# Mixture-of-experts scatter: one fp32 matmul with a weighted matrix, or two fp32r matmuls with a 0/1 matrix

## The reference

```python
    w = pg_top * pe_top / jnp.sum(pe_top, axis=-1, keepdims=True)
    eid = g_sel * EXP_PER_GROUP + e_sel
    combine = jnp.sum(jax.nn.one_hot(eid, N_EXPERTS, dtype=f32) * w[..., None], axis=1)
    hid = jax.nn.silu(jnp.einsum('td,edf->tef', t, w1)) * jnp.einsum('td,edf->tef', t, w3)
    hid = hid * combine[..., None].astype(hid.dtype)
    out = jnp.einsum('tef,efd->td', hid, w2)
    ...
    x = x + hier_moe(rms_norm(x, norm2_g), ...)
    return rms_norm(x, final_g)
```

## Time and profile before

| | us |
|---|---|
| median of 3 runs | 1282.17 (1280.4 to 1282.84) |
| span of the profiled execution | 1279.8 |
| PE busy | 1226.5 (96%) |
| DVE busy | 642.7 (50%) |
| ACT busy | 417.0 (33%) |
| DMA over the span | 263 GB/s mean |

### The profile page before, as it was taken

The page is one execution under the profiler, slowest core; times in us unless marked ns, Lnnn a source line. Parts: engine busy times, 40 slices in busy tenths (PEclk is TensorE's granted clock), DMA queues, the critical chain, the costliest instruction groups (busy, mean ns, idle before and its releaser), DMA issues.

```text
span 1279.8 us, 19040 instructions
## 1 busy us (share of the span) xinstructions
PE 1226.5 (96%) x7194; PEld 892.4 (70%) x7194; DVE 642.7 (50%) x916; ACT 417.0 (33%) x479; POOL 45.0 (4%) x57
## 2 busy tenths in 40 slices
PE   5999999999999999999999966999999999999996
PEld 4888888888888888888878866455444445544551
DVE  3678555544666656668875556122233322233224
ACT  4444333333334344343434452111111112111113
POOL 1000000001002012000000011000000000000000
PEclk9999999999999999999999987999999999999998
DMA  7655565665555445556765645999999999999991
GB/s 242 224 184 177 164 197 169 192 186 161 183 160 167 146 152 167 159 165 193 262 174 172 255 157 191 365 395 424 426 425 426 426 425 424 425 425 425 426 412 68
DMA packets 170146, 336.52 MB, mean 263 GB/s; under 512 B 12144, under 2 KB 136192, under 8 KB 153088
## 3 DMA queue, kind: packets, MB, share of 16 engines
q1 hardware_dynamic: 163088, 335.58, 70.9%
q10 hardware_dynamic: 7024, 0.48, 0.4%
HBM read 333.93 MB, written 2.11 MB: 263 GB/s over the span
## 4 chain that ended last, share of the span: by engine, by line
PE 56%; issue 39%; ACT 1%; ACTq 1%; DVE 1%; POOL 1%; DMA 0%; POOLq 0%; DVEq 0%
PE ps L819 19%; PE ps L835 11%; PE ps L821 9%; PE ps L837 5%; PE ps L968 5%; PE ps L969 2%; PE ps L808 1%; POOL h2lo L546 1%; PE ps L937 0%; PE ps L988 0%; ACTq L558 0%; DVE wsplit L1142 0%; ACT xsq L566 0%; ACT h2n L738 0%; DMA brt<-in_b_exp_dram 0%
## 5 line engine op out<-in xcount | busy, mean ns | idle before, releaser
L1142 DVE TENSOR_TENSOR wsplit<-wraw,wsplit 128x2048 fp32r<-128x2048 f32 x120 | 277.1, 2309 | 181.4 <-ACT wsplit L575 180.5
L819 PE MATMUL ps<-act_split,wsplit 128*128 128x512 f32 x1024 | 360.6, 397 | 0.0
L575 ACT ACTIVATE wsplit<-wraw 128x2048 fp32r<-128x2048 f32 x120 | 230.2, 1918 | 387.8 <-PE ps L821 204.4
L821 PE MATMUL ps<-act_split,wsplit 128*128 128x256 f32 x1024 | 286.6, 280 | 0.0
L835 PE MATMUL ps<-wsplit,act_split 128*128 128x512 f32 x640 | 228.3, 401 | 2.9 <-DVE wsplit L1142 2.9
L819 PEld LDWEIGHTS ps<-act_split,wsplit 128*128 128x128 f32 x1024 | 192.0, 188 | 46.1 <-DVE wsplit L1142 1.3
L821 PEld LDWEIGHTS ps<-act_split,wsplit 128*128 128x128 f32 x1024 | 193.3, 189 | 0.2
L837 PE MATMUL ps<-wsplit,act_split 128*128 128x256 f32 x640 | 179.6, 281 | 0.0
L1588 DVE TENSOR_TENSOR hid<-sg,ps 128x128 f32<-128x128 f32 x32 | 9.2, 288 | 268.0 <-ACT sg L763 268.0
L835 PEld LDWEIGHTS ps<-wsplit,act_split 128*128 128x128 f32 x640 | 121.0, 189 | 32.7 <-issue 2.7
L1094 PE MATMUL ps<-ys,mixT 128*128 128x512 f32 x256 | 128.7, 619 | 0.5 <-DVE x L1597 0.2
(11 more groups left out here) (267 smaller groups left out, 944.9 us busy)
## 6 DMA issues: line engine op xcount, KB each, us to landing
w_a<-in_w_dram SPq DMA_DIRECT2D x96, 1024.0 KB, 14.2
w_b<-in_w_dram SPq DMA_DIRECT2D x96, 1024.0 KB, 13.9
wraw<-in_w_in_dram SPq DMA_DIRECT2D x88, 1024.0 KB, 5.0
wraw<-in_w_out_dram SPq DMA_DIRECT2D x16, 1024.0 KB, 5.1
wraw<-in_w_branch_m_dram SPq DMA_DIRECT2D x8, 1024.0 KB, 5.1
wraw<-in_w_branch_a_dram SPq DMA_DIRECT2D x8, 1024.0 KB, 5.0
xin<-in_x_dram SPq DMA_DIRECT2D x2, 1024.0 KB, 6.4
x<-in_x_dram SPq DMA_DIRECT2D x1, 2048.0 KB, 9.4
```

What stands on the lines that cost most here:

```text
L575: act.activation(wsplit[:, q % 2, :, 0], wraw[:, q % RAW], ACT.Copy).then_inc(rounded, 1)
L819: pe.matmul(banks[b], w[:, k, 0, b * P:(b + 1) * P], a, start=first and k == 0, stop=False)
L821: last = pe.matmul(banks[b][:, 0:T], w[:, k, 1, b * P:(b + 1) * P], a[:, 0], start=False, stop=last_half and k == HALF_K - 1)
L1142: dve.tensor_tensor(wsplit[:, q % 2, :, 1], wraw[:, q % RAW], wsplit[:, q % 2, :, 0].bitcast(F32), ALU.subtract).then_inc(split, 1)
```

## The change

The scatter's matrix is split into a 0/1 matrix (slot_of) and a weight per slot (slot_w). ACT multiplies the experts' output by slot_w as it copies it out of PSUM, and rounds it to fp32r (ys_hi). DVE computes what the rounding lost (ys_lo, fp32r too) from the same bank of PSUM. PE multiplies both with slot_of, and the second matmul accumulates on the first. mixT and its copy on ACT go; slots() on DVE makes slot_w and slot_of from the transposed mix instead. Buffers are placed anew, and the semaphore ys_ready now comes from DVE, for ys_lo.

```diff
@@ -267,15 +268,20 @@
-        ys = sb("ys", [P, D], at=AT_QK + 24 * KB)
-        place["at"] = AT_SEL
-        mix = sb("mix", [P, TT, P])
-        mixT = sb("mixT", [P, T])
+        ys_hi = sb("ys_hi", [P, D], F32R, at=AT_QK + 24 * KB)
+
+        ys_lo = [sb("ys_lo_left", [P, D // 2], F32R, at=AT_TOK + 52 * KB),
+                 sb("ys_lo_right", [P, D // 2], F32R, at=AT_SEL)]
...
+        slot_w = sb("slot_w", [P, 1])
...
+        slot_of = sb("slot_of", [P, T], F32R, at=AT_PHASE + KB)
...
@@ -764,14 +770,13 @@
-                        act.wait_ge(mix_turned, s + 2)
                         act.wait_ge(scattered, s * GROUPS_OUT + 1)
-                        act.activation(mixT[:], ps[:, 1, P:3 * P], ACT.Copy).then_inc(mixT_ready, 1)
+                        act.wait_ge(slots_ready, s + 2)
                         for h in range(2):
                             act.wait_ge(y_summed, s * 2 + (h + 2))
-                            act.activation(ys[:, h * (D // 2):(h + 1) * (D // 2)],
+                            act.activation(ys_hi[:, h * (D // 2):(h + 1) * (D // 2)],
                                            ps[:, 2 + 2 * h:4 + 2 * h].rearrange("p a n -> p (a n)"),
-                                           ACT.Copy).then_inc(ys_ready, 1)
+                                           ACT.Copy, scale=slot_w[:, 0:1]).then_inc(ys_rounded, 1)
...
@@ -1088,11 +1093,13 @@
                     if g % 4 == 0:
                         pe.wait_ge(ys_ready, s * 2 + (g // 4 + 2))
-                        pe.wait_ge(mixT_ready, s + 2)
+                        pe.wait_ge(slots_ready, s + 2)
                     pe.wait_ge(added, s * GROUPS_OUT + max(1, g))
                     t, n = group_place(g)
-                    pe.matmul(ps[:, 6 + g % 2], mixT[:, t * P:(t + 1) * P],
-                              ys[:, n * 512:(n + 1) * 512], start=True, stop=True).then_inc(scattered, 1)
+                    to_tokens = slot_of[:, t * P:(t + 1) * P]
+                    pe.matmul(ps[:, 6 + g % 2], to_tokens, ys_hi[:, n * 512:(n + 1) * 512], start=True, stop=False)
+                    pe.matmul(ps[:, 6 + g % 2], to_tokens, ys_lo[n // 2][:, n % 2 * 512:(n % 2 + 1) * 512],
+                              start=False, stop=True).then_inc(scattered, 1)
...
@@ -1588,6 +1595,22 @@
+            def slots(s):
+
+                dve.wait_ge(mix_turned, s + 2)
+                dve.wait_ge(hidT_ready, s * 2 + 3)
+                dve.wait_ge(scattered, s * GROUPS_OUT + 1)
+                dve.tensor_reduce(slot_w[:], ps[:, 1, P:3 * P], AX.X, ALU.max)
+                dve.tensor_scalar(slot_of[:], ps[:, 1, P:3 * P], 0.0, None, ALU.is_gt).then_inc(slots_ready, 1)
+
+            def ys_split(s):
+
+                for h in range(2):
+                    dve.wait_ge(ys_rounded, s * 2 + (h + 1))
+                    dve.scalar_tensor_tensor(ys_lo[h][:], ps[:, 2 + 2 * h:4 + 2 * h].rearrange("p a n -> p (a n)"),
+                                             slot_w[:, 0:1], ys_hi[:, h * (D // 2):(h + 1) * (D // 2)].bitcast(F32),
+                                             ALU.mult, ALU.subtract).then_inc(ys_ready, 1)
+
...
@@ -1606,17 +1629,23 @@
                     for b in range(2):
                         silu(0, b)
+                    slots(0)
                     with steps_x.loop(1, EXPERTS // 2, 2) as i:
                         tokens_in(i, 0, i)
+                        ys_split(i - 1)
                         silu(i, 0)
                         add(i - 1, (0, 1, 2))
                         silu(i, 1)
                         add(i - 1, (3, 4, 5, 6, 7))
+                        slots(i)
+                    ys_split(EXPERTS // 2 - 1)
                     for g in range(GROUPS_OUT):
                         add(EXPERTS // 2 - 1, (g,))
```

More of the change, by code:

```diff
@@ L247, in layer @@
         iota_e = sb("iota_e", [P, EXPERTS])
+        AT_IOTA_S = place["at"]
         iota_s = sb("iota_s", [P, PAIRS])
@@ L269, in layer @@
         xe = sb("xe", [P, 2, DC, SLOTS], at=AT_QK + 16 * KB)
-        ys = sb("ys", [P, D], at=AT_QK + 24 * KB)
-        place["at"] = AT_SEL
-        mix = sb("mix", [P, TT, P])
-        mixT = sb("mixT", [P, T])
+        ys_hi = sb("ys_hi", [P, D], F32R, at=AT_QK + 24 * KB)
+        ys_lo = [sb("ys_lo_left", [P, D // 2], F32R, at=AT_TOK + 52 * KB),
+                 sb("ys_lo_right", [P, D // 2], F32R, at=AT_SEL)]
+        place["at"] = AT_SEL + 4 * KB
+        hid = sb("hid", [P, P])
         sg = sb("sg", [P, P])
-        hid = sb("hid", [P, P])
-        hidT = sb("hidT", [P, 2, P])
         spare = sb("spare", [P, 1])
+        slot_w = sb("slot_w", [P, 1])
         assert place["at"] <= AT_W2
+        mix = sb("mix", [P, TT, P], at=AT_PHASE)
+        slot_of = sb("slot_of", [P, T], F32R, at=AT_PHASE + KB)
+        hidT = sb("hidT", [P, 2, P], at=AT_IOTA_S)
         ps = ctx.enter_context(nc.psum_tensor("ps", [P, 8, 512], F32))
@@ L327, in layer @@
         upper_used = sem("upper_chunks_used")
-        mix_ready, mix_turned, mixT_ready, scattered, added = (sem(n) for n in (
-            "mix_ready", "mix_turned", "mixT_ready", "scattered", "added"))
+        mix_ready, mix_turned, slots_ready, scattered, added, ys_rounded = (sem(n) for n in (
+            "mix_ready", "mix_turned", "slots_ready", "scattered", "added", "ye_rounded"))
         fing_loaded, squares3, squares_total, out_stored, x2g_ready = (sem(n) for n in (
@@ L489, in _ @@
             for primed in (silu_done, hm_turned, ha_summed, br_lo, y_sum, y_ready, x2_ready, h_summed,
-                           mix_turned, hid_turned, hid_ready, hidT_ready, mixT_ready, y_summed, ys_ready, scattered, added):
+                           mix_turned, hid_turned, hid_ready, hidT_ready, slots_ready, y_summed, ys_ready, scattered, added):
                 pool.sem_inc(primed, 1)
@@ L1060, in turn @@
                 if b == 0:
-                    pe.wait_ge(mixT_ready, s + 1)
+                    pe.wait_ge(slots_ready, s + 1)
                 if b == 1:
@@ L1608, in experts @@
                                 silu(s, b)
+                            slots(s)
+                            ys_split(s)
                             add(s, range(GROUPS_OUT))
```

## The result

| | before | after |
|---|---|---|
| median of the runs, us | 1281.61 (1280.4 to 1282.84, 4 runs) | 1270.73 (1268.82 to 1272.52, 4 runs) |
| ratio | | 0.9921, 95% interval 0.9906 to 0.9936 |
| span of the profiled execution, us | 1279.8 | 1267.3 |

The change gains 10.1 us by the ratio (10.9 by the medians). Later sets of runs give less: the same kernel, taken again, had a median of 1274.42. How much of the 10.1 us belongs to the change is therefore part of the question.

What follows compares the result with a forecast made beforehand. PE was taken to set the pace, with the memory stream close behind. 7.1 + 0.9 + 0.3 - 1.0 = 7.3 us off the 1279.8 span gives 1272.5, plus 2.4 makes 1274.9 us; range 1271.5 to 1280.5.

Steps and rivals of the forecast that it cites:

- What bounds the kernel: Expert loop: PE sets the pace at 29.15 us an iteration; the memory stream needs 29.59 but lives off an early lead.
- What PE saves: Scatter groups in the loop: 0.38 us for groups 0 to 2 plus 0.9 for the second batch, 1.3 us an iteration.
- The cap: Last w13 quarter, hidden(15, 1): PE can gain only the loads' remaining lead, 7.1 us, not the 18.3 it saves.
- the stream's start: Start of the loop's loads: the next issue comes earlier, taken as 0.3 us gained, bounds 0 and 1.5 us.
- Behind the last wait: Scatter of groups 3 to 7 and the rows, after the last wait for loads: 0.9 us saved.
- The end: Behind the loop: both splits delay the first add by 1.3 us, 0.26 comes back; net 1.0 us lost, bounds 0.7 and 1.5.
- What was costed at nothing: In the loop: slots() on DVE, up to 1.4 us, and the two splits, 2.4 us, are hidden and cost no time.
- From span to median: Last step of the sum: the median of the runs lies 2.4 us above the profiled span, 1272.5 becoming 1274.9 us.
- Rival 1: Loop: DVE's adds and PE's sequencer hold the groups, PE saves under 0.5 us an iteration; at 0.2, 1280.2 us; chance 14%.
- Rival 2: Loop: new PE waits of 1.7 us an iteration make the clock fall; 4.8 us gained, 1277.4 us; chance 7%.
- Rival 3: Loop: the load stream can run 2.3% faster than now; gain 16.7 us, 1265.5 us; chance 2%.
- Rival 4: Loop: the load stream slows; 1.8% lower rate eats the whole gain, 2.5% gives 1285.3 us; chance 8%.

Runs made afterwards that it cites:

- Numbers 4 to 7: w13 released and loaded by quarters in the change (1276.89 us) and in before (1281.55 us); half of w2's traffic in the change (1256.67 us) and in before (1281.14 us).
- second pair of profiles: Both kernels taken once more without an edit: the change 1274.42 us, before 1281.02 us.
- number 8: The change's weighting, both splits and 0/1 matrix, but one fp32 scatter matmul per group and no low part added: 1283.00 us, ratio 1.0013 to before.
- numbers 9 and 10: The change with w2 in one 2 MB load per expert: 1274.07 us; the same with a rearranged end, GpSimd doing half the final_g products: 1271.96 us.
- number 4: The change with w13 released and loaded by quarters (512 KB, 4 KB rows) instead of halves: 1276.89 us, ratio 0.9971 to before.
- numbers 5 and 7: The kernel before with w13 loaded by quarters: 1281.55 us, ratio 0.9997; the kernel before with half of w2's traffic: 1281.14 us, ratio 0.9997.
- number 11: The change with w2 loaded in whole 8 KB rows, split by halves of the hidden width, 1 MB a load: 1269.89 us, ratio 0.9909 to before.
- number 10: The change with w2 in whole tiles, first add ahead of the last right split, GpSimd multiplying half the last groups by final_g: 1271.96 us, ratio 0.9928.

## Why the prediction was right or wrong

**What bounds the kernel: right.** Before is bound by PE with the stream close behind, and the change hands the bound to the stream. Numbers 4 to 7 show it from both sides.

**What PE saves: mis-sized, 1.77 us an iteration and not 1.3.** The step that failed is "DVE's times do not move". It held only that the first add of a batch waits for silu. In fact silu ends just before, and the add waited for PE's fp32 matmul: it starts 1005.23 - 1003.98 = 1.25 us behind the scatter's start, and 0.42 us behind the start of silu's second operation (1004.81), where in the change it is 0.20 (852.96 to 853.16). One early iteration of the change, PE and DVE:

```profile
852.13 0.50 PE L1100 MATMUL ps<-ys_hi,slot_of 128*128 128x512 f32 x1
...
852.47 0.39 PE L1101 MATMUL ps<-ys_lo_left,slot_of 128*128 128x512 f32 x1
...
852.70 0.39 PE L1100 MATMUL ps<-ys_hi,slot_of 128*128 128x512 f32 x1
...
853.16 1.28 DVE L1620 TENSOR_TENSOR x<-x,ps 128x512 f32<-128x512 f32 x2
853.90 0.50 PE L1100 MATMUL ps<-ys_hi,slot_of 128*128 128x512 f32 x1 [0.58 <-DVE x L1620]
```

The add comes 1.03 us behind the scatter's start, 0.22 earlier, and the third group with it. So groups 0 to 2 save 0.38 + 0.22 = 0.60 us and not 0.38, and the second batch saves 1.16 (5.01 to 3.85 us from its start to the rows) and not 0.9. The first group of a batch takes 0.57 us (852.13 to 852.70); from then on the matmuls stand 0.23 apart, the 0.48 for a group of the prediction. In the loop this error had no effect on the time, because the saving is capped; behind the last wait it is the 0.3 us below.

**The cap: right in kind, 7.1 and 0.3 us predicted, 8.2 measured.** The step took the lead of the last w13 quarter at the place where PE comes to it. In the change PE comes to it at 1227.55 + 3.67 = 1231.2, and it lands at 1206.3 + 24.9 = 1231.2: the lead is used up to the last tenth. The 7.1 us hold, though the wait itself shows four loads earlier, ahead of the lower half of w13 for b = 0 (1.18 us at 1221.41). There the lead before was a little smaller still, 6.7 us: landed at 1208.7 + 18.3 = 1227.0, needed at 1230.17 + 3.54 = 1233.7. The prediction did not look there. What was off is the term for the stream's start, taken as 0.3 us earlier: this quarter lands 409.6 us behind S, where it was 410.9 before, 1.3 us earlier (the last of w2 0.6, 420.3 against 420.9). Both lie in the bounds of 0 and 1.5; 7.1 + 1.3 is 8.4, and hidden(15, 1) itself was 0.2 longer. Nor did the stream run "without a break" from S on: in the first 10 us before had 351 GB/s. Over the first 30 us before moved 11.07 MB and the change 11.40, which is 0.8 us of stream (0.4 in the second pair of profiles); where the rest of the 1.3 us arose is open. The cover of 1.1 us for the right half of w2 in rows(15) was in fact thin: needed at 1238.68 + 3.5 = 1242.2, landed at 1241.9.

**Behind the last wait: 0.9 predicted, 1.2 measured**, the same undercounted batch. **The end: 1.0 lost predicted, 1.2 measured** in the change, and 1.1 when number 8 has it alone. The first add came 1248.17 - 1245.70 = 2.47 us behind the start of the last scatter, where the rows end, the 2.5 that the prediction gave. **What was costed at nothing: right**, by number 8.

**From span to median: the step that put the result outside the range.** The forecast was 4.2 us too high. Of these 0.9 are the sum (7.3 us, where the first pair of traces has 8.2), which the range would have held. "The median of the runs lies 2.4 above the span" rested on three runs of before. 23 further runs have a median of 1280.72, only 0.9 above that span: the term was 1.5 us too large, and with 0.9 in its place the lower end of the range is 1270.0, which holds the result. (The profiled spans elsewhere lie 1.5 below their own times.) The 1.9 us "for the spread of a median" came from the same three runs. But two medians of the very same kernel came out as 1270.73 and 1274.42, 3.7 us apart, and S alone moves by up to 6.2 us between executions. By that spread a range whose lower end allows for 1.9 us of luck is too narrow; the miss was 0.8 us. The last 1.8 us are the luck of the first set: its median lies on the low side of what ten runs together show, 1272.7, which lies in the range. Why this set was so low is not shown.

**The rivals.** Rival 1 (PE saves under 0.5) falls by the period of 27.38 us. Rival 2 did not come in the loop of the change, but numbers 9 and 10 show that it is real. The Trainium skill (TensorE: Matmul & The Clock Gate, "Why this matters for your kernels") warns of idle gaps between bursts; here seven of eleven waits of 1.9 to 2.4 us were followed by a fall. Rival 3, the faster stream, holds in small: 428 GB/s with long rows, worth 2 us. This is nearer the 435 GB/s that the Trainium skill (DMA: Bandwidth & Descriptors, "Where 436 GB/s comes from") gives for the ports of SBUF than the 358 it gives for loads from HBM; the measured rate decides. Rival 4 did not come by itself, since the rate stayed at 425, but number 4 shows what a slower stream costs: 5.5 to 6.1 us of the gain for 1.2% of rate. I had 1.8% for the whole gain of 7.3.

## What to carry to other kernels

When two resources are both near their end, first measure the lead of the second over the first at the last point where it is needed. This lead, and not the time saved per iteration, is what a change to the first can gain; here 25 us saved on PE became 8. After such a change look at the new bound: w2 by rows of 8 KB brings some 2 us once the loads set the pace. Long rows were not tried on the kernel before, but there neither a slower stream nor less traffic changed the time (numbers 5 and 7). And compare traces from a common event behind the part that the change does not touch, not by their spans: here a third of the difference of the first pair was luck ahead of the loop. The event has to be the same in both: an edit that moves an issue moves the count from it too, as with the quarters.

## What the runs showed of the hardware that was not expected

- **The rate follows the length of the rows even in loads of a megabyte.** w13 in 8 KB and w2 in 4 KB: 425 GB/s. All in 8 KB, with w2's loads still of 1 MB each (number 11): 428. All rows of 4 KB: 420, but there w13's loads were also half as large, and no run takes the two apart. The DMA share was full, 1.01 to 1.03, in all three.
- **Short falls of the clock come and go between executions of one program** in a stretch where PE is busy all the time (300 to 340 us: 0.96 in one execution, 1.00 in another, of the same kernel). S moves by up to 6.2 us over 14 executions. The falls make only part of it: two executions with the same granted clock up to S have it 2.4 us apart.
- **Waits of PE of 1.9 to 2.4 us in the loop were followed by a fall of the clock in seven of eleven cases; those of up to 1.8 us were not.** At the end of the change the clock fell behind a wait of 2.0 us:

```profile
1242.00:1250.00 8.00, 6.00 (x25) 2.65 (x24) 4.32 (x5) 3.35 (x5) 0.00 (x0) 0.93 0.03 14
```

```profile
1248.90 0.79 PE L1100 MATMUL ps<-ys_hi,slot_of 128*128 128x512 f32 x1 [2.00 <-DVE x L1620]
1249.49 0.63 PE L1101 MATMUL ps<-ys_lo_left,slot_of 128*128 128x512 f32 x1
```

A matmul record is 0.63 us long there instead of 0.39. DVE's adds and multiplications follow each other there every 0.60 us with hardly a gap, so it can have cost little. The wait need not be the cause: at the end of number 10 the clock fell as well, behind waits of 0.3, 1.05 and 0.4 us.
